# A hybrid decoder layer on one core: half of the late gather placed between the first pair's w2 products, and whole 2 MB expert loads from the second pair to the fourteenth

## What is computed

```
hid = jax.nn.silu(jnp.einsum('td,edf->tef', t, w1)) * jnp.einsum('td,edf->tef', t, w3)
hid = hid * combine[..., None].astype(hid.dtype)
out = jnp.einsum('tef,efd->td', hid, w2)
```

## Time and profile before

| | us |
|---|---|
| median of 3 runs (lowest to highest) | 1206.77 (1206.34 to 1207.33) |
| the profiled execution, its own time | 1206.56 |
| its span, first to last instruction | 1204.8 |
| late gather and first pair start | 744.4 |
| end of the first pair's w2 product | 774.87 |
| last matmul of the w1 and w3 products of the last pair ends | 1180.1 |

### The profile page before, as it was taken

The page is one execution under the profiler, slowest core; times in us unless marked ns, Lnnn a source line. Parts: engine busy times, 40 slices in busy tenths (PEclk is TensorE's granted clock), DMA queues, the critical chain, the costliest instruction groups (busy, mean ns, idle before and its releaser), DMA issues.

```text
span 1204.8 us, 18957 instructions
## 1 busy us (share of the span) xinstructions
PE 1173.3 (97%) x7316; PEld 886.3 (74%) x7316; DVE 700.1 (58%) x1025; ACT 378.7 (31%) x406; POOL 44.5 (4%) x52
## 2 busy tenths in 40 slices
PE   8999999999999999999999999999999999999996
PEld 8888888888888888888898888655555454545552
DVE  5788555556566767676886656444444444434445
ACT  5444433334444353543434543110011010000103
POOL 1000001001002021000000000000000000000002
PEclk9999999999999999999999999999999999999998
DMA  8665565665754554455664896999999999999996
GB/s 297 198 187 197 176 201 181 197 202 176 211 171 161 173 174 153 160 174 175 197 221 116 274 398 260 343 418 433 428 435 428 434 428 434 431 430 434 423 418 263
DMA packets 161706, 337.68 MB, mean 280 GB/s; under 512 B 13552, under 2 KB 139648, under 8 KB 148352
## 3 DMA queue, kind: packets, MB, share of 16 engines
q1 hardware_dynamic: 154544, 335.69, 74.8%
q10 hardware_dynamic: 7120, 1.42, 0.7%
HBM read 334.97 MB, written 2.12 MB: 280 GB/s over the span
## 4 chain that ended last, share of the span: by engine, by line
PE 81%; DMA 15%; DVE 1%; issue 1%; ACT 1%; POOL 0%; SPq 0%; POOLq 0%; DVEq 0%; ACTq 0%
PE ps L1061 20%; PE ps L1415 14%; DMA w_b<-in_w_dram 14%; PE ps L1091 11%; PE ps L1064 10%; PE ps L1094 6%; PE ps L1219 4%; PE ps L1447 4%; PE ps L1221 2%; PE ps L1455 1%; PE ps L1349 1%; PE ps L1460 1%; PE ps L1036 1%; DMA xin<-in_x_dram 0%; PE ps L1183 0%
## 5 line engine op out<-in xcount | busy, mean ns | idle before, releaser
L1558 DVE TENSOR_TENSOR wsplit<-wraw,wsplit 128x2048 fp32r<-128x2048 f32 x119 | 273.6, 2299 | 176.1 <-ACT wsplit L729 176.0
L729 ACT ACTIVATE wsplit<-wraw 128x2048 fp32r<-128x2048 f32 x119 | 228.1, 1917 | 366.2 <-PE ps L1064 194.1
L1061 PE MATMUL ps<-act_split,wsplit 128*128 128x512 f32 x1024 | 323.2, 397 | 0.0
L1415 PE MATMUL ps<-w_a,xe_a 128*64 128x256 f32 x960 | 219.8, 385 | 13.0 <-DMA w_b<-in_w_dram 12.7
L1064 PEld LDWEIGHTS ps<-act_split,wsplit 128*128 128x128 f32 x1024 | 192.3, 188 | 45.4
L1415 PE MATMUL ps<-w_b,xe_b 128*64 128x256 f32 x960 | 219.9, 385 | 0.0
L1415 PEld LDWEIGHTS ps<-w_a,xe_a 128*64 128x64 f32 x960 | 129.8, 138 | 98.5 <-DMA w_b<-in_w_dram 20.9
L1064 PE MATMUL ps<-act_split,wsplit 128*128 128x256 f32 x1024 | 201.3, 278 | 0.0
L1091 PE MATMUL ps<-wsplit,act_split 128*128 128x512 f32 x608 | 191.9, 397 | 0.5 <-DVE wsplit L1558 0.4
L1061 PEld LDWEIGHTS ps<-act_split,wsplit 128*128 128x128 f32 x1024 | 156.3, 189 | 0.9 <-issue 0.4
L1094 PEld LDWEIGHTS ps<-wsplit,act_split 128*128 128x128 f32 x608 | 114.2, 188 | 27.0
(11 more groups left out here) (316 smaller groups left out, 1126.3 us busy)
## 6 DMA issues: line engine op xcount, KB each, us to landing
wraw<-in_w_in_dram SPq DMA_DIRECT2D x88, 1024.0 KB, 4.9
w_a<-in_w_dram SPq DMA_DIRECT2D x37, 2048.0 KB, 15.4
w_b<-in_w_dram SPq DMA_DIRECT2D x37, 2048.0 KB, 19.5
wraw<-in_w_out_dram SPq DMA_DIRECT2D x16, 1024.0 KB, 6.1
w_a<-in_w_dram SPq DMA_DIRECT2D x14, 1024.0 KB, 12.9
w_b<-in_w_dram SPq DMA_DIRECT2D x14, 1024.0 KB, 15.4
wraw<-in_w_branch_m_dram SPq DMA_DIRECT2D x8, 1024.0 KB, 5.2
wraw<-in_w_branch_a_dram SPq DMA_DIRECT2D x8, 1024.0 KB, 5.1
```

Source lines behind the costliest of these rows:

```text
L729: act.activation(wsplit[:, q % 2, :, 0], wraw[:, q % RAW], ACT.Copy).then_inc(rounded, 1)
L1061: pe.matmul(banks[b], w[:, k, 0, b * P:(b + 1) * P], act_of(q, k), start=first and k == 0, stop=False)
L1415: last = pe.matmul(ps[b * SLOTS:(b + 1) * SLOTS, 2 * w, 0:FF], operands[b][:, k], w13[b][:, w, k], start=k == 0, stop=k == DC - 1)
L1558: dve.tensor_tensor(wsplit[:, q % 2, :, 1], wraw[:, q % RAW], wsplit[:, q % 2, :, 0].bitcast(F32), ALU.subtract).then_inc(split, 1)
```

## The change

It has three pieces.

1. **The late gather.** Before, two of its banks followed each of the parts 0, 1 and 2 of pair 0, one part 3, and one the transpose. Now one bank follows each part; then come the transpose, the first two column blocks of the w2 product, the last four banks, and the other two column blocks. ACT and DVE evict, round and sum in the matching order: ACT copies `hidT` before its third and fourth bank and rounds the left half of the product between these two; DVE multiplies `hid` before its second bank and copies expert a's places (`xe_a`) after the first piece of `x2`.
2. **The loads of pair 1 and w2 of pair 2.** The quarters, halves and column pieces are gone; from pair 1 on `next_hidden` and `next_rows` load whole matrices. In exchange pairs 1 and 2 are written out on PE ahead of its loop, since their semaphore counts are constants now.
3. **The last pair.** Parts 0, 1 and 2 are loaded in quarters of 512 KB, with a semaphore for the first quarters of each part, and PE waits in the middle of the part for the second.

```diff
@@ SP
-                sp.wait_ge(first_quarter, chunks)
-                for b in range(2):
-                    load_steps(b, 2 + b, 0, 0, DC // 4, w13_loaded[0][0])
-                parts_done(1, 0)
-                for b in range(2):
-                    load_steps(b, 2 + b, 0, DC // 4, DC // 2, w13_loaded[0][0])
-                for part in range(1, PARTS):
-                    parts_done(1, part)
-                    for b in range(2):
-                        load_part(b, 2 + b, part)
-                for n in range(4):
-                    sp.wait_ge(y_summed, 4 * (chunks - 1) + n + 2)
-                    cols = slice(n * 512, (n + 1) * 512)
-                    for b in range(2):
-                        sp.dma_start(w2s[0][b][:, :, cols], w2_v[:, 4 + b, :, cols]).then_inc(w2_loaded[0], 16)
-                for i in range(2, HALF_LEAD - 1):
+                for i in range(1, HALF_LEAD - 1):
                     next_hidden(i)
                     next_rows(i + 1, (i + 1) % 2)
...
                 for part in range(PARTS - 1):
+                    w, h = divmod(part, 2)
                     parts_done(LAST, part)
-                    for b in range(2):
-                        load_part(b, 2 * LAST + b, part)
+                    for first, loaded in ((h * PART_K, first_quarters[part]), (h * PART_K + DC // 4, w13_loaded[w][h])):
+                        for b in range(2):
+                            load_steps(b, 2 * LAST + b, w, first, first + DC // 4, loaded)
@@ ACT
                     gathered(1, (0,))
                     silu(0)
-                    gathered(1, (2, 4, 6))
+                    gathered(1, (2,))
                     turn_hidden(0)
+                    gathered(1, (4,))
+                    act.wait_ge(x2_whole, 1)
+                    ys_round(0, 0, 2)
+                    gathered(1, (6,))
                 act.wait_ge(x2_whole, 3)
                 if chunks == 1:
-                    ys_round(0, 0, 2)
                     ys_round(0, 2, 4)
@@ PE, hidden
+                    if last_pair and part < PARTS - 1:
+                        pe.wait_ge(first_quarters[part], 32)
+                    else:
+                        pe.wait_ge(w13_loaded[w][h], second_halves if h else i * 32 + 32)
                     for k in range(h * PART_K, (h + 1) * PART_K):
+                        if last_pair and part < PARTS - 1 and k == h * PART_K + DC // 4:
+                            pe.wait_ge(w13_loaded[w][h], second_halves if h else i * 32 + 32)
@@ PE, experts
-                hidden(0, 0, (xg[:, :, 0:SLOTS], xe_first), [[lambda js=js: gather_late(js)] for js in ((0, 1), (2, 3), (4, 5), (6,))])
+                hidden(0, 0, (xg[:, :, 0:SLOTS], xe_first), [[lambda j=j: gather_late((j,))] for j in range(PARTS)])
                 turn(0)
-                gather_late((7,))
+                pe.wait_ge(xg_act, N_BANKS // 2 + 2)
+                rows(0, 0, 0, (0, 1))
+                gather_late((4, 5, 6, 7))
                 pe.wait_ge(xg_act, N_BANKS)
-                rows(0, 0, 0)
+                pe.wait_ge(xg_dve, N_BANKS // 2 + 2)
+                rows(0, 0, 0, (2, 3))
...
-                with pe.Fori(0, N_PAIRS // 2 - 2) as j:
+                hidden_and_scatter(1, 0)
+                rows(0, 1, 1)
+                hidden_and_scatter(2, 1)
+                rows(1, 2, 0)
+                with pe.Fori(1, N_PAIRS // 2 - 2) as j:
@@ DVE
                 slots(0, 0)
+                gate(0)
+                up(0)
                 gathered(1, (3,))
-                gate(0)
                 make_x2(*late_chunks[0])
+                starts_at = starts_of(1, 0)
+                dve.wait_ge(x2_whole, 1)
+                copy_tokens(starts_at, 1, (0,))
                 gathered(1, (5,))
                 make_x2(*late_chunks[1])
-                up(0)
-                starts_at = starts_of(1, 0)
                 gathered(1, (7,))
                 make_x2(*late_chunks[2])
                 all_gathered()
-                copy_tokens(starts_at, 1)
+                copy_tokens(starts_at, 1, (1,))
```

More of the change, by code:

```diff
@@ L354, in layer @@
         w2_last = [sem(f"w2_last_piece{n}_loaded") for n in range(4)]
+        first_quarters = [sem(f"last_pair_part{n}_first_quarter_loaded") for n in range(PARTS - 1)]
         w2_fourteenth = [sem(f"w2_pair14_piece{n}_loaded") for n in range(4)]
@@ L358, in layer @@
                              "hidT_ready", "ye_summed", "ye_ready"))
-        first_quarter = sem("first_quarter_of_w1_used")
         tile_summed, tile_added, tile_turned, tile_copied = (sem(n) for n in (
@@ L1407, in hidden @@
                         pe.wait_ge(xe_ready, part + 1)
-                    second_halves = {0: 32, LAST - 1: 96, LAST: 128}.get(i, 64) if isinstance(i, int) else 64
-                    quarters = 32 if w == 0 and not (isinstance(i, int) and i == 0) else 0
-                    pe.wait_ge(w13_loaded[w][h], second_halves if h else i * 32 + (32 + quarters))
+                    second_halves = {LAST - 1: 64, LAST: 96}.get(i, 32) if isinstance(i, int) else 32
+                    last_pair = isinstance(i, int) and i == LAST
+                    if last_pair and part < PARTS - 1:
+                        pe.wait_ge(first_quarters[part], 32)
+                    else:
+                        pe.wait_ge(w13_loaded[w][h], second_halves if h else i * 32 + 32)
                     for k in range(h * PART_K, (h + 1) * PART_K):
-                        if isinstance(i, int) and i == LAST and w == 1 and k == DC * 3 // 4:
+                        if last_pair and part < PARTS - 1 and k == h * PART_K + DC // 4:
+                            pe.wait_ge(w13_loaded[w][h], second_halves if h else i * 32 + 32)
+                        if last_pair and w == 1 and k == DC * 3 // 4:
                             pe.wait_ge(w3_last, 32)
@@ L1416, in hidden @@
                                              start=k == 0, stop=k == DC - 1)
-                        if isinstance(i, int) and i == 0 and part == 0 and k == DC // 4 - 1:
-                            last.then_inc(first_quarter, 1)
                     last.then_inc(h_parts, 1)
@@ L1439, in rows @@
                 if pieces is None:
-                    pieces_more = 96 if slot == 0 and not (isinstance(load_no, int) and load_no == 0) else 0
-                    pe.wait_ge(w2_loaded[slot], load_no * 32 + (32 + pieces_more))
+                    pe.wait_ge(w2_loaded[slot], load_no * 32 + 32)
                 for n in ns:
@@ L1488, in experts @@
                     pair_in_chunks(0, 0, 0)
-                    with pe.Fori(0, N_PAIRS // 2 - 2) as j:
+                    pair_in_chunks(1, 0, 1)
+                    pair_in_chunks(2, 1, 0)
+                    with pe.Fori(1, N_PAIRS // 2 - 2) as j:
                         pair_in_chunks(j * 2 + 1, j, 1)
@@ L2066, in all_gathered, with copy_tokens @@
                 dve.wait_ge(xg_dve, N_BANKS)
-            def copy_tokens(starts_at, s):
+            def copy_tokens(starts_at, s, of_pair=range(2)):
                 dve.wait_ge(h_parts, s * PARTS + 1)
-                for b, at in enumerate(starts_at):
-                    dve.tensor_copy(xe[b][:], xg[:, :, ds(at, SLOTS)]).then_inc(xe_ready, 1)
+                for b in of_pair:
+                    dve.tensor_copy(xe[b][:], xg[:, :, ds(starts_at[b], SLOTS)]).then_inc(xe_ready, 1)
             def make_mix(i, c, s):
```

## The result

The changed kernel takes 1209.95 us (median of 12 runs, 1209.03 to 1210.85) against 1206.97 of the kernel before on the same chip (12 runs, 1206.05 to 1207.52). The ratio is 1.0027 with a 95% interval of 1.0019 to 1.0035: slower by 3.0 us, where I had forecast 1.7 and a range that ended 0.15 us short of it. The direction of my sum was right, its size was not: it gave a little over half of what was measured.

What follows compares the result with a forecast made beforehand. The prediction took the DMA queue as the bound, set by when pair 2's w1 lands: 1.5 us later there, last products 1.7 us later, so 1206.56 + 1.7 = 1208.2 us, range 1205.5 to 1209.8.

Steps and rivals of the forecast that it cites:

- What bounds the kernel: Whole kernel: PE leads for the first pairs, then the queue at 431 GB/s sets the pace to the end.
- every microsecond by which the queue falls behind near 785 us is paid at the end, one to one: Queue at w1 of pair 2: its lateness there, forecast 1.5 us, reaches the kernel's end in full.
- Part 1, the order on PE: Pair 0 on PE: the moved gather banks cost 0.4 us, w2 product ending at 775.2 to 775.3 against 774.87.
- Part 2, the loads: Pairs 1 and 2: late first issue and one uncovered start put w1 of pair 2 at 797.7 against 796.2.
- the start on the dry queue: W2 of pair 2, issued at 775.35: 2.9 us of start plus 9.73 of transfer, landing at 788.0.
- Of loads 3 to 13 and of pair 14 nothing changes but these 1.5 us: Middle of the run: the queue's lag of 1.5 us from pair 2 stays as it is.
- Part 3, the last pair: Last pair: quarters cost 0.45 us and win at most 0.3; products end at 1181.8 against 1180.1.
- The sum: Whole kernel: 1206.56 us of the profiled execution plus 1.7 gives 1208.2.
- The holes close: Rival, queue from 756 to 785 us: running at 431 GB/s throughout returns 4.8 us, 1201.8; chance 0.10.
- Its milder form: Rival, w2 of pair 2: a start costing nothing to 1.3 us for 2.9, giving 1205.3 to 1206.6; chance 0.10.
- PE waits for ACT: Rival, between the w2 product's halves: a late ACT delays the end equally, 1.0 us gives 1209.2; chance 0.20, shared with dearer start.
- The other half of that rival: W2 of pair 2: a start dearer than 3.2 us for 16 KB rows; chance 0.20 together with the ACT wait.

Runs made afterwards that it cites:

- loads_only: Kernel before with only the whole-matrix loads of pair 1 and of w2 of pair 2: 1209.81 us against 1207.22, ratio 1.0021.
- gather_only: Kernel before with only the new order of the late gather on PE, ACT and DVE: 1207.42 us against 1207.00, ratio 1.0006.
- no_quarters: Changed kernel with the last pair loaded in halves again: 1209.98 us against 1207.22 of the kernel before, ratio 1.0024.
- w2_8k_rows: Changed kernel with w2 of pair 2 in four 1 MB loads with 8 KB rows, same moment: 1210.04 us against 1206.79 of the kernel before.
- lead6: Changed kernel with HALF_LEAD 6 for 5, both w2 loads of pair 5 issued ahead of its w1: 1209.83 us against 1207.22 of the kernel before.
- filler13: Changed kernel with eight unread small matmuls on PE ahead of pair 13's first part: 1209.94 us against 1206.79 of the kernel before, ratio 1.0026.
- w2_pieces: Changed kernel with w2 of pair 2 in the old eight column pieces, each pair behind its column block: 1209.66 us against 1207.22 of the kernel before.
- quarters_only: Kernel before with only the last pair loaded in quarters: 1207.25 us against 1207.00, ratio 1.0003.

## Why the prediction failed

**What bounds the kernel.** Held in the main. The thirteen changed kernels fall into two groups: the nine with w1 of pair 2 at +54.3 or later end 2.6 to 4.9 us later, the four at +51.1 to +52.0 end -0.8 to +0.3. What did not hold is "every microsecond by which the queue falls behind near 785 us is paid at the end, one to one". loads_only is 3.6 us late at w1 of pair 2 and 2.6 at the end; gather_only is 1.2 behind in the middle of the run and 0.3 at the last of w3, while no_quarters, w2_8k_rows, lead6 and filler13 go from 2.3 to 2.6 up to 3.1 or 3.2. Later loads win and lose some tenths, already before: w3 of pair 2 landed 5.5 us behind w1 there (801.75 against 796.2), for 4.87. Why the tail draws the lags together no run shows.

**Part 1, the order on PE.** "The move costs PE 0.4 us": it cost 0.81. The term was taken from pairs of banks, and the three banks taken out saved 2.9 us and not 3.15; the w2 product in two halves takes 7.28 us where I halved 7.09. The wait ahead of the w2 product was sized nearly right (0.46 said, 0.52 measured). Alone the move costs the kernel nothing that can be told, but behind a dry queue its 0.8 us hold up w2.

**Part 2, the loads.** The mechanism was right: w3's landing 775.2 (776.2), w2's issue 775.3 (775.11), a dry spell near 776 with 246 GB/s, 391 and 370 ahead of it instead of the 430 that I named. The failing step is here. Mis-sized was the start on the dry queue: "775.35 + 2.9 + 9.73"; measured, 13.35 from issue to landing, so 3.6 for 2.9, although w3 was still landing in the first microsecond. So w1 of pair 2 came at +54.35 where I had 797.7 - 744.4 = +53.3: 0.4 from PE and 0.7 from the start. The queue was 2.5 us behind and not 1.5, and this one microsecond is most of what was missing: the change is 3.0 us where my sum had 1.7. (The 1208.2 fell short of the median by 0.4 more, since I started from 1206.56 and the median of the kernel before is 1206.97 here.) For the start, the Trainium skill ("DMA: Bandwidth & Descriptors", section "Anatomy of one DMA") has a fixed 2.0 us, which is little more than half of the 3.6. It gives that figure for DMAs issued by GpSimd, which I had left out; these are issued by SP, and the measured number decides.

"Of loads 3 to 13 and of pair 14 nothing changes but these 1.5 us" did not hold either: counted from the pair's start the queue went from 2.5 us behind to 3.4 at pair 5 in this execution. The trace fits the account that PE waits longer, its clock falls and the next w1 is issued with too little lead, but that account isn't shown: w2_pieces had the same half clock there (5.17 us for this part) and a lead of 4.4 us, and lost nothing. At the end it made no difference that a run shows, since kernels without this dent have the same lag at the last of w3 and the same time.

**Part 3, the last pair.** Its small size was right: quarters_only is 0.25 us above the kernel before, no_quarters 2.8, where the kernel after is 3.0 above it. The last products end at 1183.25 and not 1181.8. The waits in the middle of the parts that I named did not appear.

Chain of waits after, through the last pair:

```profile
1166.54 3.60 PE ps L1410 x32
...
1176.19 7.06 PE ps L1410 x64
1183.25 0.43 PE ps L1447
```

The last quarter of w3 lands at 1180.6, 2.6 us before the end and not 1.84: PE ran behind the data here.

**The sum.** In the profile, counted from the start of the pair, the end comes 3.8 us later. The queue's part is 3.3, its lag at the last quarter of w3 (2.5 at w1 of pair 2, 3.4 from pair 5 on). The other 0.5 is PE, which ends 2.6 us behind that landing where it was 2.1 before. This execution's first pair starts 0.6 us earlier, which leaves 3.2. The median is 3.0 later.

**The rivals.** *The holes close* fell. From 756 to 785 us the queue did move more, 385 GB/s for 360, but over the first 53.6 us of the pair 322 for 340: it was emptier than before, in another place. Its milder form, a start for 1.3 us or less, fell with the 3.6 us. *PE waits for ACT* fell as well. ACT's timeline after:

```profile
768.66 0.84 ACT L932 ACTIVATE xg<-ps,g2T 128x256 f32<-128x256 f32 x2 [5.00 <-PE ps L1339]
769.39 1.03 ACT L956 ACTIVATE ys_hi<-ps 128x1024 fp32r<-128x1024 f32 x1
770.52 0.84 ACT L932 ACTIVATE xg<-ps,g2T 128x256 f32<-128x256 f32 x2
```

ACT is done at 771.36, and PE goes on at 771.44 behind its last bank without a gap. The other half of that rival, a start dearer than 3.2 us, is what came, and w2_8k_rows shows that its reason was not the row length.

**Open.** Why a start on this queue costs 3.6 us when the issue comes one microsecond before the load ahead lands, why leads of 4.1 and 4.4 us lost nothing in some kernels, one of 4.2 us 2.0 in another and leads of 6.5 us 0.5 to 0.8, and why lags of 2.3 to 3.4 us in the middle of the run come out at 3.1 to 3.3 in the last pair in five kernels. I measured these and explain none.

## What to carry to other kernels

Where one queue sets the pace to the end, don't ask how fast its transfers are, but when the buffer that they need comes free: larger loads wait for the whole buffer, and the wait is paid at the end, while the rate they gain is only there if the queue is fed. Two edits that hold back the same landing must be undone together before either shows its cost. And the lag at one landing is not yet the lag at the end: follow it through the later landings, where some is lost and some won, before you price it or blame a dent in the middle.

## What the runs showed that I had not expected

- A whole 2 MB load issued 1.0 to 1.3 us ahead of the previous landing takes 7.3 to 7.6 us from that landing; with 6 us of lead at w1 of pair 5 it was 4.8 to 4.9. A queue that is not yet empty can already owe the price of a start.
- PE idle for 2.4 to 3.15 us is followed by half the clock (0.50 granted) in some cases and not in others: after 2.38 us it fell in the kernel after, after 2.49 us (no_quarters, in the same pair) it did not. It happens in the kernel before as well, and within one execution: there a part took 3.67 us behind 2.54 us of idle time at 938 us and 5.36 behind 2.53 at 1020. It made a part 1.5 to 1.7 us longer.
- SP's issues of the last eight quarters took 0.78 to 2.56 us each, where those of whole loads took 0.33 to 0.43 almost always; here they were far enough ahead not to matter (the last, issued at 1165.60, landed 15.0 us later). SP's timeline after:

```profile
1163.00 2.56 SPq L528 DMA_DIRECT2D w_a<-in_w_dram  x1
```
